# The block tiles' loads handed from SP's queue to Pool's in a two-layer kernel on one core

## The reference, cut to what matters

```python
def first_block(x, ...):
    p = rms_norm(x) @ w_in[2048 x 5120]           # two gated convolutions on the parts of p
    h = x + rms_norm(concat(y_a, y_b) @ w_out)
    z = square(relu(rms_norm(h) @ w_up[2048 x 8192]))
    return h + rms_norm(z @ w_down[8192 x 2048])

def hybrid_layer(x, ...):
    proj = rmsnorm(x) @ w_in_2[2048 x 12288]      # q, k, v of 16 heads, and three gates
    # 4 heads stick-breaking, 6 with block-sparse, 6 with dilated attention, then
    x = x + (sum of the three gated branch products) @ w_out_2
    gu = rmsnorm(x) @ w_gu_2[2048 x 11264]
    return x + (silu(gu[:, :5632]) * gu[:, 5632:]) @ w_down_2[5632 x 2048]
```

## Time and profile before

| | us |
|---|---|
| median of 3 runs | 2455.79 |
| the profiled execution | 2460.21 |
| its span, first to last instruction | 2458.4 |
| TensorE busy | 2441.5 |
| VectorE busy | 1818.9 |
| ScalarE busy | 1486.1 |
| Pool busy | 66.8 |
| share of DMA engines taken by SP's queue | 66.6% |
| share taken by Pool's queue | 3.2% |
| granted clock of TensorE | 0.999 |

### The profile page before, as it was taken

One profiled execution on the slowest core, in us unless ns is written; L12 is line 12 of the kernel. 1 busy time (PEld: TensorE's weight loads), 2 busy tenths in 40 slices (PEclk: granted clock), 3 DMA queues, 4 the chain that ended last, 5 costly groups with the idle time before them and its releaser, 6 DMA issues.

```text
span 2458.4 us, 28786 instructions
## 1 busy us (share of the span) xinstructions
PE 2441.5 (99%) x10849; PEld 2019.0 (82%) x10849; DVE 1818.9 (74%) x1967; ACT 1486.1 (60%) x1801; POOL 66.8 (3%) x78
## 2 busy tenths in 40 slices
PE   9999999999999999999999999999999999999999
PEld 8888888788787888888888888888888888888887
DVE  5888578778788878666667645546588888878874
ACT  6886557557467476566576645545655555564553
POOL 0110000000000000010100000000000000000000
PEclk9999999999999999999999999999999999999999
DMA  8997667768668577577757666667767657675755
GB/s 286 265 262 211 203 200 195 210 211 220 220 185 247 180 215 224 163 208 217 229 172 201 187 211 199 203 193 209 246 194 209 216 196 219 188 227 188 222 180 171
DMA packets 348562, 515.41 MB, mean 210 GB/s; under 512 B 113840, under 2 KB 114152, under 8 KB 348168
## 3 DMA queue, kind: packets, MB, share of 16 engines
q1 hardware_dynamic: 343592, 496.63, 66.6%
q0 software_dynamic: 4688, 16.93, 3.2%
q10 hardware_dynamic: 144, 0.01, 0.0%
HBM read 476.52 MB, written 4.47 MB: 196 GB/s over the span
## 4 chain that ended last, share of the span: by engine, by line
PE 87%; DVE 5%; DMA 2%; ACT 2%; issue 2%; SPq 1%; POOL 0%; ACTq 0%; DVEq 0%; POOLq 0%
PE acc L601 16%; PE acc L603 15%; PE acc L602 15%; PE acc L766 10%; PE acc L768 10%; PE acc L767 10%; DVE w_lo L1554 2%; DMA planesT_ff<-planes_ff 2%; PE acc L755 1%; PE acc L753 1%; PE acc L754 1%; ACT w_hi L970 1%; PE tp L753 1%; PE tp L755 1%; PE tp L754 1%
## 5 line engine op out<-in xcount | busy, mean ns | idle before, releaser
L1554 DVE TENSOR_TENSOR w_lo<-raw,w_hi 128x1024 fp32r<-128x1024 f32 x776 | 941.8, 1223 | 503.9 <-ACT w_hi L970 498.3
L970 ACT ACTIVATE w_hi<-raw 128x1024 fp32r<-128x1024 f32 x776 | 813.8, 1056 | 713.8 <-PE acc L603 373.9
L601 PE MATMUL acc<-w_lo,a_hi 128*128 128x512 f32 x1216 | 476.7, 392 | 0.7 <-issue 0.7
L603 PE MATMUL acc<-w_hi,a_lo 128*128 128x512 f32 x1216 | 473.6, 389 | 0.0
L602 PE MATMUL acc<-w_hi,a_hi 128*128 128x512 f32 x1216 | 473.2, 389 | 0.0
L766 PE MATMUL acc<-w_lo,a_hi 128*128 128x512 f32 x816 | 317.5, 389 | 0.0
L767 PE MATMUL acc<-w_hi,a_hi 128*128 128x512 f32 x816 | 317.5, 389 | 0.0
L768 PE MATMUL acc<-w_hi,a_lo 128*128 128x512 f32 x816 | 317.5, 389 | 0.0
L970 ACT ACTIVATE w_hi<-quad_raw 128x1024 fp32r<-128x1024 f32 x196 | 207.7, 1060 | 126.0 <-PE acc L768 73.1
L601 PEld LDWEIGHTS acc<-w_lo,a_hi 128*128 128x128 f32 x1216 | 228.3, 188 | 48.4 <-issue 1.7
L603 PEld LDWEIGHTS acc<-w_hi,a_lo 128*128 128x128 f32 x1216 | 228.2, 188 | 48.0
(11 more groups left out here) (310 smaller groups left out, 2882.8 us busy)
## 6 DMA issues: line engine op xcount, KB each, us to landing
raw<-w_in_dram SPq DMA_DIRECT2D x272, 512.0 KB, 4.5
raw<-w_down_dram SPq DMA_DIRECT2D x172, 512.0 KB, 4.3
raw<-w_gu_dram SPq DMA_DIRECT2D x136, 512.0 KB, 4.4
raw<-w_up_dram SPq DMA_DIRECT2D x100, 512.0 KB, 4.3
raw<-w_out_dram SPq DMA_DIRECT2D x64, 512.0 KB, 4.3
quad_raw<-w_down_dram SPq DMA_DIRECT2D x44, 512.0 KB, 5.8
quad_raw<-w_gu_dram SPq DMA_DIRECT2D x40, 512.0 KB, 5.7
raw<-w_branch_dram SPq DMA_DIRECT2D x32, 512.0 KB, 3.9
```

The lines of the kernel that those rows point to most:

```text
L601: nc.tensor.matmul(out, xh, wl, start=s == 0 and k == 0, stop=False)
L603: mm = nc.tensor.matmul(out, xl, wh, start=False, stop=s == n - 1 and k == KS - 1)
L970: nc.scalar.activation(w_hi[:, g % RING], src, ACT.Copy).then_inc(hi_ready, 1)
L1554: nc.vector.tensor_tensor(w_lo[:, g % RING], src, w_hi[:, g % RING].bitcast(F32), ALU.subtract).then_inc(lo_ready, 1)
```

## The change

The block tiles are issued from Pool's queue. SP's `load_pair` loses the four loads and their waits. Pool gets `load_blocks(q)`: four loads in the order tile 1, 0, 2, 3, with the same waits as before except for the first pair of either stage, where the trigger is the eighth w_lo of the plain pair ahead. In the MLP each of the twelve skew stores stands behind the four loads of a pair and no longer waits for a count of slots. In the feed-forward part all loads stand behind the root and the memset of `wide`.

```diff
-            def load_block(q, tile, src):
-
-                if q == 0:
-                    sp.wait_ge(slot_used, G_MLP)
-                    sp.wait_ge(h_ready, NCH)
-                elif q == Q_FF:
-                    sp.wait_ge(slot_used, G_FF)
-                else:
-                    g, order = G_PAIR[QUADS[q - 1]], DOWN if "down" in QUADS[q - 1][0] else UP
-                    last = ("T2", "T3", "B21", "B22")[tile]
-                    sp.wait_ge(lo_ready, g + order.index(last) + 1)
-                    sp.wait_ge(quad_sum, 4 * q)
-                sp.dma_start(quad_raw[:, tile], src).then_inc(quad_in[tile], 16)
...
-                    if following in QUADS and k in blocks:
-                        tile = blocks[k]
-                        load_block(QUADS.index(following), tile, pair_src(following, tile % 2, tile // 2))
...
+            def load_blocks(q):
+
+                for tile in (1, 0, 2, 3):
+                    if q == 0:
+                        pool.wait_ge(lo_ready, G_MLP + SPU)
+                        pool.wait_ge(slot_used, G_MLP)
+                    elif q == Q_FF:
+                        pool.wait_ge(lo_ready, G_FF + SPU)
+                        pool.wait_ge(slot_used, G_FF)
+                    else:
+                        g, order = G_PAIR[QUADS[q - 1]], DOWN if "down" in QUADS[q - 1][0] else UP
+                        last = ("T2", "T3", "B21", "B22")[tile]
+                        pool.wait_ge(lo_ready, g + order.index(last) + 1)
+                        pool.wait_ge(quad_sum, 4 * q)
+                    pool.dma_start(quad_raw[:, tile], pair_src(QUADS[q], tile % 2, tile // 2)
+                                   ).then_inc(quad_in[tile], 16)
+
             for m in range(H_SOFT):
-                pool.wait_ge(slot_used, G_MLP + 2 * SPU * (m + 1))
+                load_blocks(m)
                 pool.wait_ge(line_out, 16 * (m + 1))
                 pool.dma_start(t["skew_dram"][m], line_dram[m].unsqueeze(0).to_broadcast([P, LINE])
                                ).then_inc(line_out, 16)
+            for q in range(H_SOFT, Q_FF):
+                load_blocks(q)
...
             root(5)
             pool.wait_ge(split_lo, S_N3 + 8)
             nc.gpsimd.memset(wide[:, :, :, :], 0.0).then_inc(wide_zero, 1)
+            for q in range(Q_FF, len(QUADS)):
+                load_blocks(q)
```

More of the change, by code:

```diff
@@ L389, in tap_first, with pair_src @@
                                         cols[:, G_CBIAS + c:G_CBIAS + c + 1], ALU.mult, ALU.add)
+        def pair_src(name, unit, s):
+            stage, b, i = name
+            if stage == "up":
+                c0 = b * D + (2 * i + unit) * W
+                return w_up[:, KS * s:KS * s + KS, c0:c0 + W]
+            if stage == "down":
+                c0 = (2 * i + unit) * W
+                return w_down[:, b * KT + KS * s:b * KT + KS * s + KS, c0:c0 + W]
+            if stage == "ff down":
+                c0 = (2 * i + unit) * W
+                return w_dn2[:, b * KT + KS * s:b * KT + KS * s + KS, c0:c0 + W]
+            c0 = unit * FF2 + b * D + i * W
+            return w_gu[:, KS * s:KS * s + KS, c0:c0 + W]
         block = ctx.enter_context(nc.Block())
@@ L460, in _, with load_pair @@
                     load(w_out[:, ks(part * RING + s), c0:c0 + W])
-            def load_block(q, tile, src):
-                if q == 0:
-                    sp.wait_ge(slot_used, G_MLP)
-                    sp.wait_ge(h_ready, NCH)
-                elif q == Q_FF:
-                    sp.wait_ge(slot_used, G_FF)
-                else:
-                    g, order = G_PAIR[QUADS[q - 1]], DOWN if "down" in QUADS[q - 1][0] else UP
-                    last = ("T2", "T3", "B21", "B22")[tile]
-                    sp.wait_ge(lo_ready, g + order.index(last) + 1)
-                    sp.wait_ge(quad_sum, 4 * q)
-                sp.dma_start(quad_raw[:, tile], src).then_inc(quad_in[tile], 16)
[L476 to L493, removed]
+            def load_pair(name, turns):
                 if name in QUADS:
@@ L498, in load_pair @@
                     steps = [(unit, s) for unit in range(2) for s in range(SPU)]
-                    blocks = {k + 3: tile for k, tile in blocks.items()}
                 for k, (unit, s) in enumerate(steps):
@@ L503, in load_pair @@
                     load(pair_src(name, unit, s))
-                    if following in QUADS and k in blocks:
-                        tile = blocks[k]
-                        load_block(QUADS.index(following), tile, pair_src(following, tile % 2, tile // 2))
             mlp_pairs = [(stage, b, i) for b in range(MLP_BLOCKS) for stage in ("up", "down")
                          for i in range(2)]
-            for name, following in zip(mlp_pairs, mlp_pairs[1:] + [None]):
+            for name in mlp_pairs:
                 stage, b, i = name
@@ L517, in _ @@
                     turns = {3: [("ff", x + 2)], 9: [("ff", x + 3)]}
-                load_pair(name, following, turns)
+                load_pair(name, turns)
             for v in range(3 * NCH):
@@ L550, in _ @@
                         [("ff", b, j) for j in range(FF_PAIRS[b])] + [("ff down", b, i) for i in range(2)]]
-            for name, following in zip(ff_pairs, ff_pairs[1:-1]):
+            for name in ff_pairs[:-2]:
                 stage, b, j = name
-                if name == ("ff down", 2, 0):
-                    break
                 x, turns = X_FF + b * NCH, {}
```

## The result

The changed kernel takes 2503.89 us (median of four runs, 2496.27 to 2510.19) against 2456.07 us: 1.0194 times the time before, 95% interval 1.0166 to 1.0222. The forecast was 2459 us with a range of 2449 to 2474. It was wrong, by 45 us and to the slow side. The profiled execution took 2500.99 us, its span is 2499.2 us, 40.8 more than before, and the mean granted clock of TensorE is 0.993 against 0.999.

A forecast was written before the change was run, and what follows sets the result against it. It took TensorE's matmuls as the bound, with change only in its waits, mainly behind transposes. Terms 3.0 - 1.0 + 1.1 + 0 = +3.1 us on 2455.8 gave 2458.9, stated as 2459, range 2449 to 2474.

The forecast's parts named there:

- What bounds the kernel: TensorE: nearly all matmuls, 2441.5 of 2458.4 us; changes come in its waits, chiefly 9.3 us for b_lo, behind transposes.
- SP loses: On SP's queue ahead of the transposes: without the block tile's bytes they would be 1.4 to 1.9 us earlier.
- Pool gains: Four load issues per pair on Pool, bytes still in flight near the transposes: net +0.5 us a place, between -1.9 and +3.5.
- I take 0.6 earlier: Raw load ahead of the transposes, beside Pool's tiles: between 1.2 us earlier and 0.3 later, taken as 0.6 earlier.
- I take a third, 1.1 us: Tile 3 and the store meeting the transposes: bounds 0 and 3.2 us; most comes behind them, so 1.1 us.
- How many places: Six places at 0.5 us, +3.0; against it two starts of down pairs at -0.5 each, -1.0.
- The start of the feed-forward stage: Pool's first loads wait behind root and memset: VectorE stands 4.3 us, less 3.15 reserve, +1.1 us for TensorE.
- The first burst: Four tiles sent at once before the first up pair by block products: 0, up to 1.5 us.
- The second: Rival: tile 3 and store fall fully on the transposes at six places, about +22 us, 2478; chance 0.35 of over +4.9.
- The third: Rival: block tiles too late for their sums in every pair, against 11 us of reserve; no chance of its own.
- the sign for wrong: At TensorE's three waits for b_lo: each under 1 us or over 6 us would show the forecast wrong.
- The other sign: In the down pairs, sign for right: second transposes land within a microsecond of 8 us after their raw load.

The follow-up runs named there:

- k4: The kernel before, all loads on SP, with tile 0 issued behind the transposes and the raw load that follows them: 2448.29 us, ratio 0.9968.
- k9: The kernel before, with tile 3 of each pair alone issued from Pool, once the lower part of B22 is made: 2466.02 us, ratio 1.0034.
- k3: The changed kernel, with tile 3 (and the store behind it) waiting until the running pair's transposes have landed: 2471.13 us, ratio 1.0066.
- k6: The changed kernel, stage starts repaired, tile order 1, 0, 3, 2, every tile but tile 1 waiting for the running pair's last transposes: 2454.67 us, ratio 0.9990.
- k10: k6 with SP's second pair of transposes issued ahead of raw load 8 instead of behind it: 2449.69 us, ratio 0.9970.

## Why the prediction was wrong

*What bounds the kernel* was right: nearly everything moved in the waits behind the transposes, and k4 confirms with its 8 us.

*SP loses*, right in kind and too small (4.2 us at a place in k4, for my 1.4 to 1.9): k4 takes the block tile away from ahead of the transposes and they land in 4.1 us at that place instead of 7.95.

*Pool gains* is the step that failed, at the front term and still more at the term behind. I measure both from SP's issue of the raw load (at 435.3 us in the earlier trace rows's place), first to the landing of what stands ahead of the transposes (before tile 0, now the raw load), then from there to the landing of the second transpose. The places are named by where the wait of the changed kernel starts.

| place | ahead, before | ahead, after | behind, before | behind, after |
|---|---|---|---|---|
| 451 us | 6.1 | 7.3 | 4.1 | 6.4 |
| 629 us | 6.5 | 7.8 | 3.5 | 8.0 |
| 811 us | 6.3 | 7.5 | 2.0 | 5.1 |

- Ahead, "I take 0.6 earlier": measured 1.2 to 1.3 later. I had tiles 1 and 0 some 3 us before the raw load, tile 2 "some 2 us later", and the load delayed by one tile or two. But VectorE makes B21's w_lo right behind the sum T4 for which Pool stood 32 us, so all three tiles went out within 1.5 us, and the load stood behind all three.
- Behind, "I take a third, 1.1 us": measured 2.3, 4.5 and 3.1. "The most of it comes behind them" was right of the packets: 1984, 1547 and 1846 of the transposes' 2048 were out before tile 3's first. It was wrong as a price. What comes behind on Pool's queue still holds back the transposes' last increment: it landed 3.9, 2.6 and 2.2 us after their last data packet, right behind the store. The row for sharing had shown it: at 1217 us the slower transpose had its last data packet at 1222.5 and landed at 1224.8; I took its 3.2 us for shared packets. In k9 this cost 1.4 us a wait; that it is near my 1.1 is luck. k3, which takes it away, gives 33 us back over all places.

Together 3.5, 5.8 and 4.3 us, 13.6 for my 1.5, and the waits for b_lo grew by 13.2. My bounds were -1.9 to +3.5 a place. I had worked them out by adding two effects, each read in a stretch in which the other was absent: the row for sharing (640 KB from Pool beside two transposes) had no earlier tiles of Pool in flight. By k9 and k3 they cost 9 and 15 us in all, and 48 together.

*How many places* was too few. I had the three for b_lo, one up pair and two in the feed-forward down products. The rows for w_lo show others: a wait in the ff pairs at 1895 us and at 2159 us (4.4 and 2.1 us), where the transposes took 13.6 and 11.3 us over the two, against 7.4 and 7.0 before. They had a reserve before, and I had looked only at transposes that TensorE already waited for. The two places in the feed-forward down products, for which I had 0.5 each, cost 2.5 and 2.1 us (w_lo, at 1986 and 2246 us).

*The start of the feed-forward stage* was right in each number. Pool issues at 1805.90 behind the memset, VectorE stands 4.21 us for the tiles (4.3 forecast), and TensorE waits 1.0 us (1.1 forecast). The two tiles land 6.5 us after the first issue, as in the row, and not in the 4.4 us of the estimate beside it. Timelines of Pool and VectorE, then the waits from 1812 to 1820 us:

```profile
1805.90 2.90 POOL L2411 DMA_DIRECT2D quad_raw<-w_gu_dram  x4
```

```profile
1812.43 1.22 DVE L1497 TENSOR_TENSOR quad_raw<-quad_raw 128x1024 f32<-128x1024 f32 x1 [4.21 <-DMA quad_raw<-w_gu_dram]
```

```profile
PE acc L580 <- DVE w_lo L1533: 1.0, 1, 1.0
```

*The first burst* I took at nothing, up to 1.5 us. It cost 2.1, and 3.4 us of half clock behind it. Four tiles and a store went out from 349.06 us (timeline of Pool), the raw loads of SP beside them took 7.6 to 11.8 us, and TensorE waited (366 to 376 us):

```profile
349.06 2.96 POOL L2411 DMA_DIRECT2D quad_raw<-w_up_dram  x4
```

```profile
PE acc L580 <- DVE w_lo L1533: 2.1, 1, 2.1
```

*The clock* stood in no term. At 0.999 before it looked like nothing, yet a wait of 3.9 us already had 3.4 us at 0.5 behind it. 6.8 us of the 40.8 are this.

*The rivals.* The second had the right sign and the right actor, at 0.35 and 2478 us. It priced a place at one overlap, 3.2 us, and knew neither the places in the ff pairs nor the clock, so it was short by 26 us. Its decision point, 1.6 us behind the front, was passed at all three waits for b_lo. The third, block tiles too late for their sums, did not happen but at the head of the feed-forward part.

*The signs.* All three waits for b_lo came out over 6 us, which was the sign for wrong. The other sign, a landing within a microsecond of 8 us "after their raw load", was misread from the start: 7.95 us is the second transpose's own time. From the raw load's issue it was 10.2 us before, and it is 13.7, 15.8 and 12.6 now.

Of the Trainium skill, "DMA: Bandwidth & Descriptors", Queues, rings and completion order, the rule that each engine goes round its queues packet by packet does not describe these stretches: from 436 to 439 us of the changed kernel Pool has 258 packets and SP none, and in k9 the transposes' packets are out before tile 3's. The same section says that a transfer's closing increment lands only after every earlier write of that DMA engine, across its queues. With that the landings agree: the raw load at 442.7 behind tile 2's 441.9, the transposes at 449.0 behind the store's 448.8, in the next block at 630.17 behind 629.92, and in the 13 pairs counted under k9.

**Left open**: by what rule the packets of two queues take turns. At the places looked at they go out nearly in the order of issue, whichever the queue. The raw load's first packet comes behind 316 of the 384 packets of Pool's three loads (266 and 297 at the other two places), 4.1 us after its issue, where a raw load with nothing ahead has its first after 1.0. Tile 3's first comes behind most of the transposes' packets. No run was made to test this, nor why an increment waits for a load that was issued later. At 629 us some of the loss is also in the data: the last 126 of the transposes' 2048 packets go out from 624 to 628 us, among tile 3's.

## What to carry to other kernels

A transfer that an engine is waiting for should have nothing bulky in flight, in its own queue or in another: ask at its issue what was issued in the 3 us before and will be in the 5 us after. A second queue takes the order away that the first one gave for nothing: here a load issued there after a transfer still held back its landing. So loads moved there need a wait for the transfer they must not pass (k6, k10). And a long wait of TensorE can cost more than its length: in the twelve traces here, half clock came with every wait of 2.9 us and more, and with some of 2.0 to 2.5.

## What the runs showed of the hardware

- Pool's three loads of 512 KB, 433 to 442 us, kept a load of SP's queue, issued at 435.3, without a packet until 439.4; the load took 7.3 us instead of 4.7.
- 256 KB transposes (1024 packets of 256 bytes each) land in 4.1 us with only a raw load ahead (k4, first place), and in up to 12.2 us with Pool's loads around.
- The last increment of a pair of transposes landed 0.5 to 0.7 us after the last data packet in all 26 pairs of k4, and 1.9 to 3.9 us after it in 13 of 26 in the changed kernel, 0.2 to 0.4 us behind a later transfer of Pool.
- The issue of a pair's first transpose holds SP for 1.24 us in most cases, and for 2.8 to 3.2 us at the three places of the changed kernel, with Pool's loads in flight; that of the second for 2.0 to 2.5 us there in k4, and for 3.4 to 4.0 in the changed kernel.
- The granted clock was 0.5 in stretches of 3.4, 6.8 and 10.2 us in the changed kernel: 3.4 with waits of 2.1, 2.5 and 4.4 us, 6.8 with waits of 6.4 and 6.6, 10.2 with the one of 9.5. Two more waits of 2.1 us had none. In k4, where no wait is over 1.0 us, it never fell before the end.
